# Second mixer of a two-block network: gates and branches with features on the partitions

## The reference, cut to what matters

```python
def second_block(x, c, ...):                       # x: 1 x 256 x 1024
    ...
    h = rms_norm(x, norm1_g) * (1 + scale1) + shift1
    proj = h @ w_in                                # width 4 * 512 + 2 * 1024
    q, k, v, u, z_gate = jnp.split(proj, split_pts, axis=-1)
    y_attn = moba_attention(q, k, v, rel_bias) @ w_branch_attn     # 512 -> 1024
    y_pool = pool_mixer(u, pool_w, pool_scale) @ w_branch_pool     # 512 -> 1024
    g_attn, g_pool = jnp.split(jax.nn.sigmoid(z_gate + b_gate), 2, axis=-1)
    mixed = (g_attn * y_attn + g_pool * y_pool) @ w_out            # 1024 -> 1024
    x = x + gate1 * mixed
    h2 = rms_norm(x, norm2_g) * (1 + scale2) + shift2
    y_moe = hier_moe(h2, ...)                      # 32 experts, 6 MB of weights each
    x = x + gate2 * y_moe
    return rms_norm(x, norm_f_g)
```

## Time and profile before

| | us |
|---|---|
| median of three runs | 1412.61 |
| the three runs | 1412.36 to 1413.67 |
| the profiled execution | 1414.97 |
| its span | 1413.2 |
| TensorE busy in the span | 1170.1 |
| VectorE busy | 358.8 |
| ScalarE busy | 182.0 |

### The profile page before, as it was taken

How to read it: one execution, slowest core, us unless ns; L and a number is a source line. 1 busy time by engine, 2 the same in 40 slices (tenths; PEclk the granted TensorE clock), 3 DMA queues, 4 the chain that set the end, 5 groups by cost and what they waited for, 6 DMA issues and landing times.

```text
span 1413.2 us, 21012 instructions
## 1 busy us (share of the span) xinstructions
PE 1170.1 (83%) x8910; PEld 601.7 (43%) x8910; DVE 358.8 (25%) x941; ACT 182.0 (13%) x371; POOL 87.4 (6%) x118
## 2 busy tenths in 40 slices
PE   5999999999999999899879999898366563665637
PEld 3664455655555555455438444454022221212212
DVE  1598575411111111111112244333010000100002
ACT  1210124211111111111121013021000000000000
POOL 2498000000000000000000000000000000000000
PEclk9999999999999999999998999999777877778778
DMA  9979974789999999999992413938999999999995
GB/s 388 347 291 430 408 331 189 293 337 422 419 419 420 420 421 420 420 420 420 420 427 82 197 69 148 393 130 366 429 427 428 429 427 427 427 429 428 426 425 223
DMA packets 51802, 507.81 MB, mean 359 GB/s; under 512 B 6445, under 2 KB 7637, under 8 KB 11001
## 3 DMA queue, kind: packets, MB, share of 16 engines
q1 hardware_dynamic: 49689, 503.07, 85.5%
q10 hardware_dynamic: 2016, 3.36, 0.7%
HBM read 505.34 MB, written 1.06 MB: 358 GB/s over the span
## 4 chain that ended last, share of the span: by engine, by line
PE 57%; DMA 26%; SPq 10%; DVE 3%; issue 2%; ACT 1%; POOL 0%; DVEq 0%; POOLq 0%; ACTq 0%
SPq L637 8%; PE PS L1607 7%; DMA W<-in_w_expert_gate 6%; PE PS L1783 6%; PE PS L1127 4%; DMA W<-in_w_expert_up 4%; PE PS L1676 4%; PE PS L1617 4%; PE PS L1468 4%; PE PS L1442 3%; PE PS L1797 3%; PE PS L1073 3%; DMA hx<-in_w_expert_up 2%; DMA hx<-in_w_expert_down 2%; PE PS L1148 2%; DMA scr<-in_w_expert_up 2%
## 5 line engine op out<-in xcount | busy, mean ns | idle before, releaser
L1783 PE MATMUL PS<-W,scr 128*32 128x512 f32 x640 | 143.7, 721 | 84.7 <-DMA W<-in_w_expert_gate 21.2
L1783 PE MATMUL PS<-scr 128*32 128x512 f32 x288 | 108.9, 727 | 64.2 <-DMA W<-in_w_expert_gate 33.6
L2312 DVE TENSOR_TENSOR scr<-scr,PS 128x256 f32<-128x256 f32 (+1 forms) x33 | 23.4, 711 | 521.4 <-PE PS L1783 263.6
L1607 PE MATMUL PS<-W,scr 128*32 128x256 f32 (+1 forms) x1968 | 140.2, 387 | 10.8 <-DMA W<-in_we_up 8.3
L1468 PE MATMUL PS<-scr 128*128 128x512 f32 x248 | 114.7, 605 | 0.0
L1607 PEld LDWEIGHTS PS<-W,scr 128*32 128x32 f32 (+1 forms) x1968 | 79.2, 116 | 71.0 <-issue 14.0
L1783 PEld LDWEIGHTS PS<-W,scr 128*32 128x32 f32 x640 | 34.7, 130 | 148.7 <-issue 102.1
L1442 PE MATMUL PS<-scr 128*128 128x128 bf16 x1536 | 92.6, 221 | 0.0
L918 ACT COPY scr<-PS 128x512 f32<-128x512 f32 x66 | 38.5, 585 | 414.0 <-PE PS L1442 410.2
L1442 PEld LDWEIGHTS PS<-scr 128*128 128x128 bf16 x1536 | 90.1, 99 | 0.9 <-issue 0.6
L1797 PE MATMUL PS<-W,scr 128*32 128x512 f32 x288 | 67.9, 691 | 13.9 <-DMA scr<-in_w_expert_down 7.2
(11 more groups left out here) (441 smaller groups left out, 1442.9 us busy)
## 6 DMA issues: line engine op xcount, KB each, us to landing
W<-in_we_up SPq DMA_DIRECT2D x47, 1024.0 KB, 23.3
W<-in_we_gate SPq DMA_DIRECT2D x44, 1024.0 KB, 23.4
W<-in_w_ada SPq DMA_DIRECT2D x10, 4096.0 KB, 13.8
W<-in_w_expert_gate SPq DMA_DIRECT2D x20, 2048.0 KB, 29.5
W<-in_w_expert_up SPq DMA_DIRECT2D x20, 2048.0 KB, 29.4
W<-in_we_down SPq DMA_DIRECT2D x39, 1024.0 KB, 23.6
W<-in_w_expert_down SPq DMA_DIRECT2D x16, 2048.0 KB, 32.6
scr<-in_w_expert_gate SPq DMA_DIRECT2D x10, 2048.0 KB, 26.0
```

What stands on the lines that cost most here:

```text
L1607: m = mm(PS[4 + kind][at:at + size, 0:F1], hTe[:, k, at:at + size], piece_view((g, kind, j))[:, k, :], start=(k == 0), stop=(k == KD - 1))
L1783: m = mm(PS[4 + kind][j * CAP2:(j + 1) * CAP2, :], hTe[:, k, j * CAP2:(j + 1) * CAP2], piece_view2((g, kind, j))[:, k, :], start=(k == 0), ...
```

## The change

Gates and branches are computed with the weights as stationary operand, and `hT`, `oT2` and `plT2` as the moving one, 256 columns (all tokens) at a time. A gate n is now a half and a quarter q of the features, two blocks of 128 features side by side in one bank; `zgT` holds the gates with features on the partitions. Since the bias is then one number for each partition, ScalarE adds it as it reads the bank (`branch_gate_out`); its values are 16 more columns of `cols`, the broadcast of `bgrow` falls away, and so does VectorE's addition. ScalarE does this after the exponentials of each pair for the first six gates, and takes the sigmoid of them afterwards; for the last two it takes the sigmoid straight from PSUM.

The branches go through four quarters q of the features, the pool branch ahead of the attention branch, in banks of their own (`BRANCH_BANKS`); only the first attention quarter waits for `attn_done`. VectorE mixes a quarter and writes it to `hT` as the output projection wants it. The output projection, unchanged in its operands, waits for one quarter before each second block of its first 512 columns.

```diff
+BRANCH_BANKS = ((4, 5, 6, 7), (2, 3, 0, 1))
...
-        zg = c2(NB, 2 * D)
+        zgT = c2(2, KD, T)
...
-                    sp.dma_start(bgrow, A["b_gate_2"][0].partition_broadcast(P)).then_inc(S["band_loaded"], 16)
...
-            for h in range(HEADS2):
-                act.wait_ge(S["smax_ready"], h + 1)
-                for b in range(NB):
...
-            for n in range(8):
-                act.wait_ge(S["zg_biased"], n + 1)
-                half, b, h = n // 4, n // 2 % 2, n % 2
-                q = slice(half * D + h * 512, half * D + h * 512 + 512)
-                step(a.activation(zg[:, b, q], zg[:, b, q], ACT.Sigmoid), S["zg_ready"], wait=False)
+            def branch_gate_out(n, func, sem):
+
+                half, q = divmod(n, 4)
+                if q == 3:
+                    act.wait_ge(S["stream2_used"], 3 + half)
+                else:
+                    act.wait_ge(S["zg_mm"], 3 * half + q + 1)
+                for m in range(2):
+                    block = 2 * q + m
+                    step(a.activation(zgT[:, half, block, :], PS[6 + n % 2][:, m * T:(m + 1) * T], func,
+                                      bias=cols[:, C_BGATE + KD * half + block:C_BGATE + KD * half + block + 1]), sem if m else None, wait=False)
+
+            for pair in range(HEADS2 // 2):
+                for h in (2 * pair, 2 * pair + 1):
+                    act.wait_ge(S["smax_ready"], h + 1)
+                    for b in range(NB):
...
+                if pair < 3:
+                    for n in (2 * pair, 2 * pair + 1):
+                        branch_gate_out(n, ACT.Identity, S["zg_biased"])
+
+            act.wait_ge(S["zg_biased"], 6)
+            for n in range(6):
+                half, q = divmod(n, 4)
+                step(a.activation(zgT[:, half, 2 * q:2 * q + 2, :], zgT[:, half, 2 * q:2 * q + 2, :], ACT.Sigmoid), S["zg_ready"], wait=False)
+            for n in (6, 7):
+                branch_gate_out(n, ACT.Sigmoid, S["zg_ready"])
...
-                half, b, h = n // 4, n // 2 % 2, n % 2
-                if n % 4 == 0:
+                half, q = divmod(n, 4)
+                if q == 0:
                     loaded2(2 + half)
                 if n >= 2:
                     pe.wait_ge(S["zg_biased"], n - 1)
-                for k in range(KD):
-                    last = mm(PS[6 + n % 2][:, :], hT[:, k, b * P:(b + 1) * P], w2k[2 + half][:, k, h * 512:(h + 1) * 512],
-                              start=(k == 0), stop=(k == KD - 1))
+                for m in range(2):
+                    for k in range(KD):
+                        last = mm(PS[6 + n % 2][:, m * T:(m + 1) * T], w2k[2 + half][:, k, (2 * q + m) * P:(2 * q + m + 1) * P], hT[:, k, :],
+                                  start=(k == 0), stop=(k == KD - 1))
...
-            pe.wait_ge(S["attn_done"], 1)
-            for n in range(4):
-                b, h = n // 2, n % 2
-                for br, src in ((0, oT2), (1, plT2)):
-                    for k in range(4):
-                        last = mm(PS[4 * br + n][:, :], src[:, k, b * P:(b + 1) * P], w2k[4][:, 4 * br + k, h * 512:(h + 1) * 512],
-                                  start=(k == 0), stop=(k == 3))
-                last.then_inc(S["stream2_used"] if n == 3 else S["proj_mm"], 1)
-
-            pe.wait_ge(S["mixed_ready"], 1)
-            for k in range(KD):
-                for b in range(NB):
-                    last = tr(PS[k // 2][:, (k % 2) * T + b * P:(k % 2) * T + (b + 1) * P], xn[:, b, k * P:(k + 1) * P], ident[:])
-                if k % 2:
-                    last.then_inc(S["mixedT_mm"], 1)
-            pe.wait_ge(S["mixedT_ready"], 4)
+            for q in range(4):
+                if q == 2:
+                    pe.wait_ge(S["zg_ready"], 8)
+                for bank, br, src in ((BRANCH_BANKS[1][q], 1, plT2), (BRANCH_BANKS[0][q], 0, oT2)):
+                    if q == 0 and br == 0:
+                        pe.wait_ge(S["attn_done"], 1)
+                    for m in range(2):
+                        block = slice((2 * q + m) * P, (2 * q + m + 1) * P)
+                        for k in range(4):
+                            last = mm(PS[bank][:, m * T:(m + 1) * T], w2k[4][:, 4 * br + k, block], src[:, k, :], start=(k == 0), stop=(k == 3))
+                last.then_inc(S["stream2_used"] if q == 3 else S["proj_mm"], 1)
+
             pe.wait_ge(S["stream2_loaded1"], 16 * 3)
             for n in range(4):
                 b, h = n // 2, n % 2
                 for k in range(KD):
+                    if n == 0 and k % 2 == 0:
+                        pe.wait_ge(S["mixedT_ready"], k // 2 + 1)
...
-                step(v.tensor_tensor(zg[:, b, q], PS[6 + n % 2][:], bgrow[:, q], ALU.add), S["zg_biased"])
...
-            for n in range(4):
-                b, h = n // 2, n % 2
-                dve.wait_ge(S["proj_mm"], 20 + n) if n < 3 else dve.wait_ge(S["stream2_used"], 5)
-                q, q2 = slice(h * 512, h * 512 + 512), slice(D + h * 512, D + h * 512 + 512)
-                step(v.tensor_tensor(xn[:, b, q], PS[n][:], zg[:, b, q], ALU.mult))
-                step(v.tensor_tensor(zg[:, b, q2], PS[4 + n][:], zg[:, b, q2], ALU.mult))
-                step(v.tensor_tensor(xn[:, b, q], xn[:, b, q], zg[:, b, q2], ALU.add))
-            dve.sem_inc(S["mixed_ready"], 1)
             for q in range(4):
-                dve.wait_ge(S["mixedT_mm"], q + 1)
-                step(v.tensor_copy(hT[:, 2 * q:2 * q + 2, :], PS[q][:].rearrange("p (k t) -> p k t", k=2)), S["mixedT_ready"])
+                dve.wait_ge(S["proj_mm"], 20 + q) if q < 3 else dve.wait_ge(S["stream2_used"], 5)
+                two = slice(2 * q, 2 * q + 2)
+                for br in range(2):
+                    step(v.tensor_tensor(zgT[:, br, two, :], PS[BRANCH_BANKS[br][q]][:].rearrange("p (k t) -> p k t", k=2), zgT[:, br, two, :], ALU.mult),
+                         wait=br == 1)
+                step(v.tensor_tensor(hT[:, two, :], zgT[:, 0, two, :], zgT[:, 1, two, :], ALU.add), S["mixedT_ready"])
```

More of the change, by code:

```diff
@@ L994, in _ @@
             act.dma_start(gate[:, 1, 0:KD * 36], A["w_routers_2"]).then_inc(S["wr_loaded"], 16)
-            for h in range(HEADS2):
-                act.wait_ge(S["smax_ready"], h + 1)
-                for b in range(NB):
-                    q = slice(0, P) if b == 0 else slice(P, P + T)
-                    step(a.activation(pexp[:, h % 2, q], pexp[:, h % 2, q], ACT.Exp, bias=st[:, 2 * (h % 2) + b:2 * (h % 2) + b + 1],
-                                      accum_out=st[:, 4 + 2 * (h % 2) + b:5 + 2 * (h % 2) + b]), S["sexp_ready"])
@@ new lines, in _ @@
+            for pair in range(HEADS2 // 2):
+                for h in (2 * pair, 2 * pair + 1):
+                    act.wait_ge(S["smax_ready"], h + 1)
+                    for b in range(NB):
+                        q = slice(0, P) if b == 0 else slice(P, P + T)
+                        step(a.activation(pexp[:, h % 2, q], pexp[:, h % 2, q], ACT.Exp, bias=st[:, 2 * (h % 2) + b:2 * (h % 2) + b + 1],
+                                          accum_out=st[:, 4 + 2 * (h % 2) + b:5 + 2 * (h % 2) + b]), S["sexp_ready"])
+                if pair < 3:
+                    for n in (2 * pair, 2 * pair + 1):
+                        branch_gate_out(n, ACT.Identity, S["zg_biased"])
@@ L1656, in _ @@
             pe.wait_ge(S["in2_ready"], 8)
-            pe.wait_ge(S["band_loaded"], 32)
+            pe.wait_ge(S["band_loaded"], 16)
             for gq in range(4):
@@ L2477, in _ @@
             for pair in range(HEADS2 // 2):
-                branch_gate(2 * pair)
-                branch_gate(2 * pair + 1)
                 if pair:
```

17 lines of the change are left out of this document (4 added, 13 removed).

## The result

| | before | changed |
|---|---|---|
| median of five runs each, us | 1412.61 | 1405.60 |
| lowest to highest | 1412.27 to 1414.36 | 1404.64 to 1405.69 |
| profiled execution (span) | 1414.97 (1413.2) | 1405.66 (1403.8) |

The medians are 7.0 us apart, a quotient of 0.9950. The ratio of the runs on record is 0.9936 (95%: 0.9921 to 0.9950), a gain of 9.0 us (7.1 to 11.2). Later sets of 19 to 31 runs of the kernel before had medians of 1414.3 to 1415.4, so its first median was a low one, and I go by the ratio: on the scale of the first median it makes 1403.6 us. So two questions stand.

What follows compares the result with a forecast made beforehand. The second mixer was taken as bound by TensorE and its waits, the experts by their weight stream, whose start moves with the mixer. -5.97 - 0.72 + 0.5 = -6.2 us gave 1406.4 us against 1412.61; 80% range 1404.0 to 1409.5.

Steps and rivals of the forecast that it cites:

- The 5.97 us of mixing, transposes and copies: Between branch projections and output projection: VectorE mixing, sixteen transposes and four copies leave the path, -5.97 us.
- The cover: Output projection: its own passes, 5.2 us, hide the fourth quarter's mixing; without that it would cost 2.2 us.
- The 0.72 us of `attn_done`: Before the branch projections: TensorE's wait for VectorE's copy goes, as the pool branch runs first, -0.72 us.
- The width, 0.5: Gates and branches: 256 instead of 512 columns, with twice the weight loads, cost +0.5 us.
- Rival D: Gates and branches: weight loads no longer hidden, so slower; 1442.4 us with none of 192 hidden; 3%.
- ScalarE, 0: Gates' eviction moved from VectorE to ScalarE: hidden by slack, costed at 0; bound 2.7 us.
- Rival B: Mixer waits not hidden: fourth quarter's mixing shows (2.2 us) or ScalarE is late (up to 2.7); 1408.6 to 1411.3; 8%.
- The stream: Experts' weight loads from 969.76 us run at DMA's rate, so the mixer's gain moves their start and the end equally.
- Rival C: Weight loads of 943.8 to 969.8 us are themselves the limit, so the end stays at 1412.6; 3%.
- the clock's dip: Between output projection and experts' stream: granted clock 0.50 from 956 to 958 us, costing 1.8 us; change in it uncertain.
- the time ahead of the mixer: Stages before the second mixer: no term; only a spread of about 1.2 us, from executions and groups' entries, was allowed.
- 10% for each side: Chance that the clock's dip changes: gone, 1404.6 us, or longer, 1408.2 to 1410; 10% each.

Runs made afterwards that it cites:

- a4: Changed kernel, output projection waiting at its start for all four mixed quarters, plus five unused VectorE additions before the last quarter's sum; 1416.7 us, ratio 1.0016 to the kernel before.
- a3: Changed kernel, but the output projection waits at its start for all four mixed quarters; 1410.3 us, ratio 0.9970 to the kernel before.
- b1: Changed kernel with the attention branch ahead of the pool branch in each quarter; 1410.7 us, ratio 0.9957 to the kernel before.
- b2: Changed kernel with gates and branches in 512 columns, activations stationary, so the mixer's values differ; 1408.1 us, ratio 0.9945 to the kernel before.
- a1: The kernel before, run again unchanged; 1413.9 us, ratio 0.9998.
- c1: a4 with TensorE's wait filled by six matmuls of 512 columns that nothing reads; 1413.9 us, ratio 0.9998 to the kernel before.
- a2: The changed kernel, run again unchanged; 1406.3 us, ratio 0.9941 to the kernel before.
- b4: Changed kernel with the 1 MB broadcast of the gates' bias put back, read by nobody; 1405.4 us, ratio 0.9923 to the kernel before.
- b5: Kernel before with the 16 more columns in the early load, read by nobody; 1414.5 us, ratio 0.9992 to the kernel before.
- d4: The kernel before, run again unchanged for a third profile; 1412.8 us, ratio 0.9989 to other runs of the same kernel.
- d1: Kernel before with each 512-column matmul of gates and branches split into two of 256; 1413.0 us, ratio 0.9983 to the kernel before.
- d2: Same kernel as d1, for a second profile; 1413.6 us, ratio 0.9992 to the kernel before.
- c4: Kernel before with only the pool branch put ahead of the attention branch, which alone waits for attention's output; 1412.9 us, ratio 0.9994 to the kernel before.
- c2: Changed kernel with the first pool branch quarter ahead of the last pair's attend; 1405.4 us, ratio 0.9945 to the kernel before.
- d3: Same kernel as b2, for a second profile; 1408.9 us, ratio 0.9959 to the kernel before.
- c3: Kernel before with unread 256-column matmuls in four TensorE gaps from 878 to 915 us, mixed_ready given by quarter; 1414.0 us, ratio 0.9993 to the kernel before.

## Why the prediction was wrong: the mechanism held, two terms stood at nothing

**The 5.97 us of mixing, transposes and copies: right.** They are gone. a4, with a wait of 5.90 us put back, loses them again. The cover is there too: a3 shows the 2.25 us that it hides.

**The 0.72 us of `attn_done`: right as a term.** b1 has 0.72 again, and loses more than that.

**The width, 0.5: right** (0.48). Rival D, weight loads no longer hidden, is out: b2 and the changed kernel, at half the width, are 0.48 us apart in the mixer.

**ScalarE, 0: right.** 3.96 us idle before the last gate; TensorE waits for no eviction. Rival B is out.

**The stream: right.** From L to the end it is 443.1 to 443.8 us in every kernel with the reference's numbers, while L lay anywhere from 958 to 972 us. Rival C would have kept the end where it was.

These terms gave 6.2; the traces without a dip have 6.6 from Q to L. Most of the 0.4 between them is a term that the prediction didn't have. The output projection's first 48 passes take 20.87 us in the kernel before and in a1, and 20.84 in a3 and c1, each time behind a wait; they take 20.60 in the changed kernel, a2, b1, b2 and b4, where they follow the branches without one. That is 0.27. Another 0.1 is the width, 0.42 against the kernel before instead of 0.5.

**The step that failed: the sum holds 0 for the clock's dip and 0 for the time ahead of the mixer.** The first is the larger fault of reasoning, the second the larger number.

**The dip: left out of the sum.** The prediction gave "10% for each side" that it changes, on the ground that "TensorE's own gaps ahead of it are the same as before". They weren't the same: the change had removed the two gaps from 880 to 915. And the dip is a thing of the execution: the kernel before and its equals with the same gaps (b5, a1, d4, d1, d2, and c4, whose gap ahead of the branches is gone) show one in 5 of 7 traces, the four with a gap put back into the new arrangement in 4 of 4 (c1's mostly filled), the arrangement without those gaps (changed, a2, b4, c2, b2, d3) in 2 of 6, c3 not. Where one dip is in the trace it cost 0.8 to 1.5 us, where two are, 2.0 to 4.7. The mean of "beyond" is 0.8 us over the first seven and 0.4 over the six. A term for it was owed: about -0.4, on the side of the gain. Idleness is a likely part of the cause, but not shown to be it: the counts are small, and c1, c2 and d3 speak against its being all. In every 3 us stretch with a clock below 1.00 DMA was busy 0.82 of the time or more, as it was around most of the gaps, and no run parts the two.

**The time ahead of the mixer: left at 0.** The prediction has no term for the stage ahead, and took 1.2 us as its own spread. In the traces Q lies at 747.6 to 749.0 in the five of the kernel before with its own width (before, a1, d4, b5, c4), mean 748.3, and at 744.8 to 748.8 in the eight of the new arrangement in 256 columns, mean 747.0. So 1.4 us of the gain come from code that is the same. It isn't the broadcast (b4: 746.1) nor the wide columns (b5: 749.0). That the matmuls' number or width decides it is spoken for by d1 and d2 (746.0, 747.7) and against by b2 and d3 (746.0, 746.3). The changed kernel alone spans 2.0 us between two executions. The cause stays open, and with so few traces I can't say how much of the 1.4 is one at all.

**Together.** By the means of nearly the same traces (before, a1, b5, c4, d4 against changed, a2, b4, c2; c4 and c2 are each 0.7 to 0.8 us shorter by their own edit) the spans are 1412.66 and 1403.22, 9.4 apart: 2.2 ahead of Q, 7.2 from Q to L, 0 behind. The ratio's 9.0 agrees. With the eight traces, Q's part is 1.4 and the sum 8.6. So what was argued from the rows is two thirds to three quarters of what was measured. That the forecast's time of 1406.4 lies 0.8 us from the changed kernel's median of 1405.6 is luck: the gain was 2.8 us too small, and the three runs that it was taken from lay some 2 us below the 104 later ones.

## What to carry to other kernels

Take a wait out of the dependent chain by letting the consumer wait for portions, in the order in which the producer ends them: here it gave the wait's length, and the cover could be worked out from two rows. Price a gap of TensorE by its length and by a chance that the clock falls behind it, and read such a dip from several executions before treating it as a property of the kernel. Where a few us are the question, put the scatter of the stage ahead, and of the baseline itself, into the range.

## What the runs showed of the hardware

- After, or in, a gap of TensorE of 0.7 to 5.9 us the granted clock was 0.50 (1.2 GHz) for some us in some executions, and not in others of the same kernel: before and a1 are the same program, with and without. A dip also came some 40 us later, with 28 us of unbroken matmuls between, in the router (a3), whose own gaps of 0.4 to 1.1 us the kernels without a dip have too.
- The first 48 passes of one projection took 20.84 to 20.87 us behind a wait of TensorE (before, a1, a3, c1) and 20.60 without one (changed, a2, b1, b2, b4), all at a granted clock of 1.00.
- Behind b1's wait of 0.72 us the clock was down within matmuls that had no gap; they took 1.73 us more. A 32-bit transpose of 128x128 took 272 ns at full clock and 418 behind such a fall.
- Whether weights or activations are stationary made no difference to these 32-bit passes: 14.01 us for 64 passes of 256 columns either way (changed kernel, d1).
- The weight stream of the experts, 443 us long, repeats to 0.7 us over 16 traces, while the end of the first 748 us scatters by 4 (744.8 to 749.0).
